# An expert loop on Trainium2 whose first three turns also hold the routing products, with a tree of comparisons and two weight loads asked for later

## The reference, cut to what matters

```python
def hierarchical_moe(h, w_rg, b_rg, w_re, b_re, w_gate, w_up, w_down):
    lg = (t @ w_rg).astype(f32) + b_rg.astype(f32)
    g_idx = jnp.argmax(lg, axis=-1)                       # 1 of 4 groups
    ...
    top_v, top_i = lax.top_k(le_sel, TOP_K_INNER)         # 2 of the 4 experts of the group
    ...
    for gi in range(N_GROUPS):
        sl = slice(gi * EXPERTS_PER_GROUP, (gi + 1) * EXPERTS_PER_GROUP)
        hid = jax.nn.silu(jnp.einsum('td,edf->etf', t, w_gate[sl])) * jnp.einsum('td,edf->etf', t, w_up[sl])
        hid = hid * combine[:, sl].T[:, :, None]
        out = out + jnp.einsum('etf,efd->td', hid, w_down[sl])
```

## Time and profile before

| | before |
|---|---|
| runs, us | 645.37, 646.57, 643.96 (median 645.37) |
| the profiled execution, us | 644.0 |
| its span (first to last instruction), us | 642.2 |
| PE busy | 578.1 us, 90% of the span |
| DVE, ACT, POOL busy | 45%, 29%, 11% |
| chain that ended last | PE 70%, DMA 14%, DVE 7%, issue 4% |
| DMA | 151.5 MB; busy 1.0 of the 16 engines' time from 343 to 556 us |
| mean granted TensorE clock | 0.964 of full speed |

### The profile page before, as it was taken

How to read it: one execution, slowest core, us unless ns; L and a number is a source line. 1 busy time by engine, 2 the same in 40 slices (tenths; PEclk the granted TensorE clock), 3 DMA queues, 4 the chain that set the end, 5 groups by cost and what they waited for, 6 DMA issues and landing times.

```text
span 642.2 us, 9631 instructions
## 1 busy us (share of the span) xinstructions
PE 578.1 (90%) x3460; PEld 379.6 (59%) x3461; DVE 288.5 (45%) x627; ACT 186.8 (29%) x414; POOL 72.0 (11%) x111
## 2 busy tenths in 40 slices
PE   9999999999999999995489999997997776888994
PEld 8988877878989999995223223232232221235883
DVE  4521365456254333275135454543532333565753
ACT  5622255546443543331000000000000000343774
POOL 0000000000000000002113223232232222210000
PEclk9999999999999999989599999998997889989998
DMA  9852213212120159569278999999999999715001
GB/s 309 216 213 86 79 54 131 66 63 70 67 66 31 36 217 423 214 222 420 100 278 338 421 417 421 419 420 421 421 420 420 422 421 412 278 65 231 33 34 65
DMA packets 45586, 151.52 MB, mean 236 GB/s; under 512 B 8296, under 2 KB 27632, under 8 KB 35056
## 3 DMA queue, kind: packets, MB, share of 16 engines
q1 hardware_dynamic: 41520, 139.77, 55.5%
q0 software_dynamic: 3744, 11.02, 4.4%
q10 hardware_dynamic: 288, 0.27, 0.2%
HBM read 141.61 MB, written 9.45 MB: 235 GB/s over the span
## 4 chain that ended last, share of the span: by engine, by line
PE 70%; DMA 14%; DVE 7%; issue 4%; ACT 2%; SPq 2%; DVEq 0%
PE bank L1634 15%; DMA ring_gu<-in_w_up 13%; PE bank L1371 13%; PE bank L1373 12%; PE bank L1372 12%; PE bank L1654 8%; PE bank L1453 2%; PE bank L1426 2%; DVE ple_lo L1302 2%; SPq L590 1%; PE bank L1467 1%; DMA gmix<-in_norm_mix 1%; PE bank L1555 1%; PE bank L1436 1%; PE bank L1591 1%
## 5 line engine op out<-in xcount | busy, mean ns | idle before, releaser
L1634 PE MATMUL bank<-ring_gu,rowsT 128*64 128x512 f32 (+1 forms) x800 | 151.1, 623 | 25.5 <-DMA ring_gu<-in_w_up 21.1
L1634 PEld LDWEIGHTS bank<-ring_gu,rowsT 128*64 128x64 f32 (+1 forms) x800 | 45.9, 132 | 128.8 <-issue 102.4
L885 ACT ACTIVATE silu_g<-bank 128x256 f32<-128x256 f32 x20 | 7.7, 385 | 247.1 <-PE bank L1634 247.1
L1654 PE MATMUL bank<-ring_dn,hidT 128*64 128x512 f32 (+1 forms) x400 | 74.2, 604 | 4.5 <-DVE hidT L1256 4.2
L1275 DVE STREAM_TRANSPOSE rowsT<-rows 128x512 f32<-128x512 f32 x21 | 23.4, 1113 | 115.4 <-PE bank L1634 109.5
L1084 DVE TENSOR_TENSOR w_lo<-w_raw,w_hi 128x2048 fp32r<-128x2048 f32 x17 | 39.0, 2292 | 76.8 <-ACT w_hi L751 65.0
L1256 DVE STREAM_TRANSPOSE hidT<-hid 32x128 f32<-32x128 f32 x160 | 64.2, 402 | 1.9
L1371 PE MATMUL bank<-w_hi,hT_hi 128*128 128x256 f32 x192 | 55.4, 289 | 0.8 <-issue 0.6
L1373 PE MATMUL bank<-w_hi,hT_lo 128*128 128x256 f32 x192 | 54.3, 283 | 0.0
L1372 PE MATMUL bank<-w_lo,hT_hi 128*128 128x256 f32 x192 | 54.3, 283 | 0.0
L1654 PEld LDWEIGHTS bank<-ring_dn,hidT 128*64 128x64 f32 (+1 forms) x400 | 22.3, 128 | 54.1 <-issue 54.1
(11 more groups left out here) (218 smaller groups left out, 906.0 us busy)
## 6 DMA issues: line engine op xcount, KB each, us to landing
ring_gu<-in_w_gate SPq DMA_DIRECT2D x32, 1024.0 KB
ring_gu<-in_w_up SPq DMA_DIRECT2D x32, 1024.0 KB
ring_dn<-in_w_down SPq DMA_DIRECT2D x16, 2048.0 KB, 19.6
w_raw<-in_w_in SPq DMA_DIRECT2D x13, 1024.0 KB, 5.0
w_raw<-in_w_out SPq DMA_DIRECT2D x4, 1024.0 KB, 4.9
ple_gate_raw<-in_w_ple_gate SPq DMA_DIRECT2D x4, 1024.0 KB, 30.4
yg<-y_rows SPq DMA_DIRECT2D x8, 512.0 KB, 7.2
xr<-in_x SPq DMA_DIRECT2D x4, 512.0 KB, 8.8
```

The lines of the kernel that those rows point to most:

```text
L1634: last = T.matmul(b_gu[q * BLK + t:q * BLK + t + n, :], rowsT[:, k, t:t + n], ring_gu[s][:, :, k, q * UC:(q + 1) * UC], start=(k == 0), st ...
L1654: last = T.matmul(b_dn[q * BLK + t:q * BLK + t + n, :], hidT[:, kf, t:t + n], ring_dn[s][:, kf, q * (D // 2):(q + 1) * (D // 2)], start=(k ...
```

## The change

Three parts, all in the stretch between the last output projection and the first expert block, and in how PE finds a variant.

1. The rank products and the list products move into the loop, as branches of turns 1 and 2. The loop has three more turns (`EARLY = 3`); a register `limit`, 1 in turn 0, 3 in turn 1, and from turn 2 on the number of blocks plus 4 (loaded after `table_ready`), says which parts of a turn are done. Ahead of the loop a directive aligns its first instruction to 256 instruction words, with padding instructions that are executed. Codes are doubled; the first four entries of `step_code` are constants, copied early, and odd: an odd code is led by the comparisons to a variant and finds that it isn't it. In turn 0 PE goes to down variant 0, in turn 1 to gate-up variant 3 and down variant 0, in turn 2 to gate-up variant 0 and down variant 4, in turn 3 to block 0's gate-up and down variant 0. The eight products of ones behind `table_ready` go, and the 14 behind the rank products become 8.
2. `one_of` halves the range of variants at each comparison and ends with one comparison for equality.
3. SP asks for down weights 2 and 3 together, after `table_ready`, the transposes of `p_sb` and the first two blocks' gathered rows.

```diff
-CODE_DN, CODE_GU_LOADS, CODE_DN_LOADS = 8, 128, 1024
-NO_GU, NO_DN = 2 * N_GU, 2 * N_DN
+CODE_DN, CODE_GU_LOADS, CODE_DN_LOADS = 16, 256, 2048
+EARLY_CODES = [(1, 1), (1, 1), (2 * 3 + 1, 2 * 4 + 1), (1, 1)]
+TURNS = 32
...
-            sp.wait_ge(s_h2, 16 * (NT + 1))
-            load_dn(3)
-
             sp.wait_ge(table_ready, 1)
             sp.wait_ge(p_T, D_PLE // P)
+            for buf in range(ROW_BUFS):
+                sp.wait_ge(s_rows[buf], 32)
             load_dn(2)
+            load_dn(3)
...
+                V.tensor_scalar(turn_limit[:], steps_r[:, N_EXPERTS - 1:], EARLY + 1 - ROUND, None, ALU.add)
...
+            dve.wait_ge(s_const, 16)
+            V.tensor_copy(step_code[:, 0:EARLY + 1], early_codes[0:1]).then_inc(early_ready, 1)
...
-            pe.wait_ge(rows_ready, 1)
-            total = pe.value_load(cum_i[0:1, N_EXPERTS - 1:N_EXPERTS], min_val=N_EXPERTS // 2, max_val=MAX_BLOCKS)
-
-            def one_of(products, number, n, pair=0):
-
-                with pe.If(number == pair):
-                    products((pair // 2, (pair + 1) // 2 % n))
-                if pair + 1 < 2 * n:
-                    with pe.Else():
-                        one_of(products, number, n, pair + 1)
+            def one_of(products, number, n, first, end):
+
+                if end - first == 1:
+                    with pe.If(number == 2 * first):
+                        products((first // 2, (first + 1) // 2 % n))
+                    return
+                mid = (first + end) // 2
+                with pe.If(number < 2 * mid):
+                    one_of(products, number, n, first, mid)
+                with pe.Else():
+                    one_of(products, number, n, mid, end)
...
-            with pe.Fori(0, MAX_BLOCKS + 2) as turn:
-                with pe.If(turn < total + 2):
-                    with pe.If(turn < total + 1):
-                        gate_up(turn, code_of(turn + 1))
-                    down(turn, code_of(turn))
-                    with pe.If(turn < 1):
+            pe.wait_ge(early_ready, 1)
+            limit = pe.alloc_register("turn_limit")
+            pe.reg_mov(limit, 1)
+            pe.wait_ge(x1_add, NT * OUT_UNITS)
+            kept_warm(14)
+            pe.addr_align(256)
+            with pe.Fori(0, EARLY + MAX_BLOCKS + 1) as turn:
+                with pe.If(turn < EARLY):
+                    with pe.If(turn == 1):
+                        ranks()
+                        pe.reg_mov(limit, EARLY)
+                    with pe.If(turn == 2):
+                        rows_of_slots()
                         pe.wait_ge(table_ready, 1)
-                        kept_warm(8)
+                        pe.reg_load(limit, turn_limit[0:1, 0:1])
+                last = pe.snap(limit, min_val=1, max_val=EARLY + 1 + MAX_BLOCKS)
+                with pe.If(turn < last):
+
+                    step = (turn + (TURNS + 1 - EARLY)) % TURNS
+                    with pe.If(turn + 1 < last):
+                        gate_up(step, code_of(turn + 1))
+                    down(step, code_of(turn))
+
+            total = pe.value_load(cum_i[0:1, N_EXPERTS - 1:N_EXPERTS], min_val=N_EXPERTS // 2, max_val=MAX_BLOCKS)
```

More of the change, by code:

```diff
@@ L60 @@
 QUADS = P // GRP
-SMALL = 2 * P + 4 + 64 + GROUPS + 8 + P + 16 + 2
+EARLY = 3
+SMALL = 2 * P + 4 + 64 + GROUPS + 8 + P + 16 + 2 + EARLY + 1
 HALF = D // 2
@@ L208, in shape_constants @@
         np.concatenate([s // GRP + QUADS * SEQ, s // BLK + 2 * N_PAIRS], 1),
+        np.tile([gu + CODE_DN * dn for gu, dn in EARLY_CODES], (P, 1)),
     ], 1).astype(np.float32)
@@ L260, in trunk @@
         (ident, tri, iota4, first_slots, grp_marks, ring_marks, minus_slot, pair_rows,
-         row_offset) = [small[:, a:a + w] for a, w in zip(starts, widths)]
+         row_offset, early_codes) = [small[:, a:a + w] for a, w in zip(starts, widths)]
         subln_b = at("subln_b", 98.25, [P, P])
@@ L310, in trunk @@
         cum_i = tiny("cum_i", [1, N_EXPERTS + 1], I32)
[L311 removed]
+        step_code = tiny("step_code", [1, EARLY + 2 + MAX_BLOCKS], I32)
+        turn_limit = tiny("turn_limit", [1, 1], I32)
         dqT = at("dqT", 124, [P, HEADS, SEQ])
@@ L1580, in kept_warm @@
                     T.matmul(b_proj[2][:, 0:P], ones[:], ones[:], start=True, stop=True)
-            pe.wait_ge(x1_add, NT * OUT_UNITS)
-            kept_warm(14)
-            pe.wait_ge(member_ready, 1)
-            T.matmul(b_rank[:, 0:80], ones[:], prefix[:].rearrange("p i e -> p (i e)"), start=True, stop=False)
-            T.matmul(b_rank[:, 0:64], tri, member[:, 1:].rearrange("p i e -> p (i e)"), start=False, stop=True).then_inc(rank_done, 1)
-            kept_warm(14)
-            for w in range(2):
-                pe.wait_ge(slot_oh_ready, 1 + w)
-                for n in range(2 * NT):
-                    last = T.matmul(b_rows[w],
-                                    slot_oh[:, n, :], blk_rows[:, w, n, :],
-                                    start=(n == 0), stop=(n == 2 * NT - 1))
-                last.then_inc(rows_done, 1)
@@ L1596, in _, with ranks @@
-            pe.wait_ge(s_pple, 16)
-            for c in range(D_PLE // P):
-                for t in range(NT):
-                    last = T.transpose(b_score[c][:, t * P:(t + 1) * P], p_sb[:, t, c * P:(c + 1) * P], ident)
-                last.then_inc(p_T, 1)
-            kept_warm(8)
-            pe.wait_ge(rows_ready, 1)
-            total = pe.value_load(cum_i[0:1, N_EXPERTS - 1:N_EXPERTS], min_val=N_EXPERTS // 2, max_val=MAX_BLOCKS)
-            def one_of(products, number, n, pair=0):
-                with pe.If(number == pair):
-                    products((pair // 2, (pair + 1) // 2 % n))
-                if pair + 1 < 2 * n:
-                    with pe.Else():
-                        one_of(products, number, n, pair + 1)
+            def ranks():
+                pe.wait_ge(member_ready, 1)
+                T.matmul(b_rank[:, 0:80], ones[:], prefix[:].rearrange("p i e -> p (i e)"), start=True, stop=False)
+                T.matmul(b_rank[:, 0:64], tri, member[:, 1:].rearrange("p i e -> p (i e)"), start=False, stop=True).then_inc(rank_done, 1)
+                kept_warm(8)
@@ new lines, in rows_of_slots @@
+            def rows_of_slots():
+                for w in range(2):
+                    pe.wait_ge(slot_oh_ready, 1 + w)
+                    for n in range(2 * NT):
+                        last = T.matmul(b_rows[w],
+                                        slot_oh[:, n, :], blk_rows[:, w, n, :],
+                                        start=(n == 0), stop=(n == 2 * NT - 1))
+                    last.then_inc(rows_done, 1)
+                pe.wait_ge(s_pple, 16)
+                for c in range(D_PLE // P):
+                    for t in range(NT):
+                        last = T.transpose(b_score[c][:, t * P:(t + 1) * P], p_sb[:, t, c * P:(c + 1) * P], ident)
+                    last.then_inc(p_T, 1)
+                kept_warm(8)
@@ L1618, in column_tiles, with gate_up @@
                 return [(q, g * GRP, GRP, slots[g]) for g in range(2) for q in range(2)]
-            def gate_up(turn, code):
+            def gate_up(step, code):
                 loads = code // CODE_GU_LOADS % (CODE_DN_LOADS // CODE_GU_LOADS)
                 def products(slots):
-                    pe.wait_ge(xT_ready, turn)
-                    pe.wait_ge(hid_ready, turn)
+                    pe.wait_ge(xT_ready, step)
+                    pe.wait_ge(hid_ready, step)
                     for k in range(KD):
@@ L1639, in products, with down @@
                     last.then_inc(gu_done, 1)
-                one_of(products, code % CODE_DN, N_GU)
-            def down(turn, code):
+                one_of(products, code % CODE_DN, N_GU, 0, 2 * N_GU)
+            def down(step, code):
                 loads = code // CODE_DN_LOADS
                 def products(slots):
-                    pe.wait_ge(hidT_ready, turn)
-                    pe.wait_ge(y_ready, turn)
+                    pe.wait_ge(hidT_ready, step)
+                    pe.wait_ge(y_ready, step)
                     pe.wait_ge(s_dn[slots[0]], 16 * loads + 16)
```

14 lines of the change are left out of this document (6 added, 8 removed).

## The result

| | before | after |
|---|---|---|
| runs, median us | 645.7 (643.96 to 646.57) | 664.9 (663.59 to 667.04) |
| the profiled execution, us | 644.0 | 663.75 |
| its span, us | 642.2 | 661.9 |
| ratio, 95% interval | | 1.0304 (1.0265 to 1.0343) |
| ranks start | 287.20 | 304.54 |

Slower by 3.0%, 19.2 us between the medians; the forecast was +7 (652.4, and 638 to 659 as the whole range), so the direction was right and the size was not. The page, against the earlier trace rows: three packets more on PE's instruction queue.

The account below looks back on a forecast made before the run. PE's wait for instruction fetches behind the table was taken to delay block 0, whose start sets the end. Terms -10.7 + 13.0 + 1.8 + 1.8 + 1.8 = +7.7 us, giving 652.4 us, range 638 to 659.

Parts of the forecast that it names:

- The wait behind the table: From table ready to block 0's first product: 7.2 us of sequencer work in place of 17.9, -10.7 us.
- The tree and the down weights: Halving comparisons in the loop, and down weights 2 and 3 loaded later: 0 us each.
- Block 0's gate and up products: Without products of ones ahead they may run wholly at the lower clock: +1.8 us, bounds 0 to 2.
- in either direction: Claim that the kernel's end moves one for one with block 0's start, whether earlier or later.
- Turn 1 at nothing: The sum held no term for fetches in turn 1, ahead of the list products.
- what was fetched stayed: Reading of 22 packets for a program with 22 working turns: instructions once fetched remain held on PE.
- rival 3: A jump out of sequence discards fetched packets; head and second packet come twice, +15 us, 660; chance 0.05 with two others.
- more than 7 fetches between 284 and block 0: Listed sign, on PE's instruction fetches before block 0, that the forecast is wrong.
- The ranks: Rank products wait for padding and turn 0's two fetches, starting at 300.2 in place of 287.2: +13.0 us, bounds +5 and +17.
- The clock: PE idle from 287 to 300, so ranks and list products run partly at the lower clock: +1.8 us, 0 to 4.
- Behind the loop and to the end: Five unused turns and the load of the number of blocks delay the embedding products: +1.8 us, bounds 0.5 to 2.5.
- Rival 5: Nothing fetched stays; fetches come again behind the table, 10.7 us, so +18.4 us in all, 664; chance 0.01.

Follow-up runs that it names:

- e5: Kernel before the change with only the tree of comparisons (part 2) added: median 644.3 us, ratio 0.999 to the kernel before.
- e6: Kernel before the change with only down weights 2 and 3 loaded behind the table and first gathered rows: median 644.1 us, ratio 0.999.
- e11: e10 with 8 products of ones of 512 columns in place of 14 of 128 behind the ranks: 641.5 us, ratio 0.995 to the kernel before.
- e2: Changed kernel with turn 1 visiting gate-up variant 0, in the first packet, in place of variant 3: 662.5 us, ratio 1.028 to the kernel before.
- e3: Changed kernel with turn 0 visiting gate-up variant 3, then down variant 0, and turn 1 staying in the first packet: 658.6 us, ratio 1.020.
- e10: e8 with the loads of expert 2's gate and up and of down 3 behind the first gathered rows: 643.4 us, ratio 0.998 to the kernel before.
- e4: Changed kernel with the rank products and their products of ones ahead of the loop again: 659.5 us, ratio 1.022 to the kernel before.
- e7: Kernel before with ranks and list products inside turn 0, touching every packet in order while DVE computes, loop head not aligned: 650.7 us, ratio 1.009.
- e8: e7 with the loop head aligned to a packet by one branch over padding: 642.4 us, ratio 0.997 to the kernel before.
- e12: e11 with the weight loads where the kernel before has them: 642.6 us, ratio 0.997 to the kernel before.
- e1: Changed kernel with one branch over the padding in place of 122 executed padding words: 658.7 us, ratio 1.021 to the kernel before.
- e9: Changed kernel with the edits of e1, e3 and e4 at once: 660.1 us, ratio 1.023 to the kernel before.

## Why the prediction was wrong

**Held.** What bounds the kernel, and that the end follows a later block 0: the stretch is 247.2 against 246.5. The wait behind the table: 7.0 us, predicted 7.2 (term -10.7, measured -10.9). That turn 0 moves ahead of the ranks, uncovered, and that this makes it slower. The tree and the down weights at nothing (e5, e6). Block 0's gate and up products: +0.5, within 0 to 2, though the term was +1.8. What did not hold is "in either direction": block 0 10.2 us earlier in e11 gave about 3 us.

**Wrong, in order of size.**

1. *Turn 1 at nothing: +5.6.* The step that failed is "what was fetched stayed", read from the earlier trace rows and carried over from a walk in order to one with jumps. The prediction named the mechanism as rival 3 (0.05 with two others) but thought that the head and the second packet come twice; by their times and the words' places it is the fourth, the fifth and the one asked for behind it. Its own sign, more than 7 fetches between 284 and block 0, came true with 8. e2 and e3 show it.
2. *The ranks: +17.3 in place of +13.0, past its upper bound of 17.* Of the 4.3 us: padding 3.0 (the head at 292.7 in place of 289.7, some 121 words at 0.072 in place of 107 at 0.05; the spacing of register operations in the earlier trace rows, 0.1, was the nearest row and nearer than the value taken); the first jump 1.2 (6.4 for 5.2); the sequencer's work ahead of it 0.5 (1.4 for 0.9). The second fetch was nearly right, 3.2 us from entering the fourth packet (300.45) to the end of the second long comparison (303.68), for 3.6.
3. *The clock: +4.3 in place of +1.8.* Ranks and DVE's wait for them 1.0, lists 3.3: all of the list products ran at the lower level. The wait in turn 1 (point 1) kept PE idle in front of them too, but that is not shown to be the reason: without that wait they take 4.88 us in e2 and again 7.07 in e3. The products of ones behind the ranks, 8 in place of 14, may have a part; no run tests them alone.
4. *Behind the loop and to the end:* +0.7 in the last down, +0.8 up to the embedding products, +1.3 in the last stage: 2.8 us, where 1.8 was predicted for all and 2.5 was the bound. The unused turns and the load, which the term consisted of, are the 0.8; the rest goes with a lower clock, 0.60 for 0.68 in the last down and 0.72 from 605 to 611, where the clock before was 1.00 from 569 to 637.

Sum: table +27.2 where +14.8 was meant. Rival 5's number (664) was nearly met, by luck, for another reason: its fetches were to come behind the table, where no comparison was long. The rule behind it (the Trainium skill, Runtime: NRT & Kernel Launch, Instruction fetch mechanics: a taken branch outside the two lines held stalls) is not what the trace shows: turns 2 and 3 cross from the first packet to the fourth and fifth with comparisons of 0.07 to 0.22 us. But its warning about jumps out of the held lines was worth more than the 0.01 that the prediction gave it and the 0.05 of rival 3: nothing in the trace of before held a jump past a packet that had not been fetched, and where no row shows the case, a chance of one in five would have been due.

## What to carry to other kernels

Touch a long loop's instructions in program order, each packet once, before the turn that counts; a visit that skips packets is paid again as soon as a skipped one is entered. Put the walk behind work that another engine does and not ahead of the first product that the others wait for, and branch over padding instead of executing it. Count what the walk costs in the clock too: PE idle during fetches runs the next products at half speed, and a start that is 10 us earlier is worth only what the stream of weights behind it can follow, and less what the same edit costs behind the loop (3 us here).

## What the runs showed of the hardware that was not expected

- A padding instruction on PE costs 0.072 us though its own work is 13 ns; 121 cost 8.7 us, and a branch over them 0.35.
- A comparison that waits for a packet of 16 KB took 2.4 (e10), 3.0 (e11) and 3.6 us (e4) with DMA idle, and 5.1 to 5.6 (before, e5, e7, e8, e12) or 7.0 (e1) with DMA at a share of 0.96 to 1.0. Full DMA is not all: 3.2 (e9) and 4.1 us (e6) were seen at 0.99. A comparison that jumps from the second packet to the down part took 4.5 (e3), 4.6 (changed) and 5.1 us (e1) with DMA idle.
- What was fetched out of order is lost when a packet in between is entered (8 fetches, 5 in order), but not by jumping back to the head. Which packet each fetch brought is inferred from its time and the words' places; the traces give only the times.
- The place of packet edges in a loop that is itself the same is worth about 8 us (e7 against e8) where fetches lie on the path.
